# Hybrid mixer tail: first attention group's logits beside the last value panel, products reordered, norm statistics per token tile

## The reference

```python
q, k = rope(cq @ w_q_up), rope(k_att)                 # 8 attention heads of 64
mask = top-64 keys of the index scores, causal        # from idx_score
p   = softmax(where(mask, q k^T / 8, -inf))           # per query and head
att = rms_norm(p @ v, attn_out_norm)                  # norm over each head's 64
W   = exp(decay matrix - row maximum)                 # 4 mLSTM heads of 128
S   = (q_m k_m^T) * 128^-0.5 * W
hm  = (S @ v_m) / max(|sum S|, exp(-M))
hm  = sigmoid(o_m) * rms_norm(hm, mlstm_out_norm)     # norm over each head's 128
y   = concat([att, hm]) @ w_out
```

## Time and profile before

| | us |
|---|---|
| median of 3 runs | 2291.05 (2290.8 to 2296.16) |
| profiled execution, its own time | 2288.99 |
| span of its trace | 2287.2 |
| TensorE busy | 2053.7 (90%) |
| VectorE busy | 1509.9 (66%) |
| ScalarE busy | 899.6 (39%) |

### The profile page before, as it was taken

How to read it: one execution, slowest core, us unless ns; L and a number is a source line. 1 busy time by engine, 2 the same in 40 slices (tenths; PEclk the granted TensorE clock), 3 DMA queues, 4 the chain that set the end, 5 groups by cost and what they waited for, 6 DMA issues and landing times. The chain is left out here.

```text
span 2287.2 us, 40136 instructions
## 1 busy us (share of the span) xinstructions
PE 2053.7 (90%) x16866; PEld 1839.9 (80%) x16866; DVE 1509.9 (66%) x2313; ACT 899.6 (39%) x1331; POOL 140.4 (6%) x231
## 2 busy tenths in 40 slices
PE   5998987999999788799987999797799989878997
PEld 5786865888887676689876999797689979877997
DVE  6866476997775666656635777777576656946444
ACT  3436443322222422322234444555344455544443
POOL 0100000010100011200210000000000000000000
PEclk7999998999999789899997999899799989979999
DMA  8531033555541554000003777332357734313552
GB/s 331 201 124 56 1 111 110 174 198 180 202 170 69 205 177 175 20 3 3 3 20 111 259 277 270 110 135 93 111 194 278 276 114 150 129 56 111 184 183 92
DMA packets 59133, 323.94 MB, mean 142 GB/s; under 512 B 6384, under 2 KB 7536, under 8 KB 32624
## 3 DMA queue, kind: packets, MB, share of 16 engines
q1 hardware_dynamic: 33360, 228.97, 28.1%
q0 software_dynamic: 25344, 92.29, 11.3%
q10 hardware_dynamic: 288, 0.66, 0.1%
HBM read 320.84 MB, written 1.05 MB: 141 GB/s over the span
## 5 line engine op out<-in xcount | busy, mean ns | idle before, releaser
L370 DVE TENSOR_TENSOR w_low<-raw,w_high 128x1024 fp32r<-128x1024 f32 (+1 forms) x408 | 473.1, 1202 | 239.3 <-ACT w_high L362 239.0
L362 ACT ACTIVATE w_high<-raw 128x1024 fp32r<-128x1024 f32 (+1 forms) x408 | 402.1, 1034 | 382.8 <-PE banks L400 374.4
L541 DVE SCALAR_TENSOR_TENSOR mod_rows<-mod_rows,silu_condition 128x1024 f32<-128x1024 f32 x176 | 212.5, 1221 | 50.7 <-DMA mod_rows<-rows_dram 48.0
L398 PE MATMUL banks<-ffn_a_l,w_high 128*128 128x256 f32 x704 | 199.9, 284 | 1.9 <-DVE ffn_hidden L996 1.9
L399 PE MATMUL banks<-ffn_a_h,w_high 128*128 128x256 f32 x704 | 199.2, 283 | 0.0
L400 PE MATMUL banks<-ffn_a_h,w_low 128*128 128x256 f32 x704 | 199.1, 283 | 0.0
L398 PE MATMUL banks<-mlp_a_l,w_high 128*128 128x512 f32 (+1 forms) x512 | 176.8, 345 | 11.7 <-DVE mlp_a_l L683 7.7
L527 POOL DMA_DIRECT2D mod_rows<-rows_dram x176 | 93.2, 530 | 1412.5 <-DVE mod_rows L541 1194.9
L399 PE MATMUL banks<-mlp_a_h,w_high 128*128 128x512 f32 (+1 forms) x512 | 175.6, 343 | 0.0
L400 PE MATMUL banks<-mlp_a_h,w_low 128*128 128x512 f32 (+1 forms) x512 | 175.4, 343 | 0.0
L398 PE MATMUL banks<-mlp_hidden_l,w_high 128*128 128x512 f32 (+1 forms) x512 | 173.4, 339 | 1.3 <-DVE mlp_hidden_l L1004 1.3
(11 more groups left out here) (595 smaller groups left out, 4891.4 us busy)
## 6 DMA issues: line engine op xcount, KB each, us to landing
raw<-panels_dram SPq DMA_DIRECT2D x204, 1024.0 KB, 4.8
mod_rows<-rows_dram POOLq DMA_DIRECT2D x176, 512.0 KB, 5.1
mod_0a_rows<-rows_dram SPq DMA_DIRECT2D x8, 1024.0 KB, 20.0
x_features<-x_features_dram SPq DMA_DIRECT2D x1, 2048.0 KB, 11.2
constants<-small_dram SPq DMA_DIRECT2D x1, 1672.5 KB, 6.8
silu_condition<-conditions_dram SPq DMA_DIRECT2D x2, 512.0 KB, 12.4
out_dram<-x_features SPq DMA_DIRECT2D x4, 256.0 KB, 2.1
constants<-small_dram SPq DMA_DIRECT2D x1, 736.5 KB, 5.1
```

The costliest lines, as they stand in the source:

```text
L362: self.nc.scalar.activation(self.wh[:, m % 2, cols], self.raw[:, slot, cols], ACT.Copy).then_inc(self.w_high, 1)
L370: self.nc.vector.tensor_tensor(self.wl[:, m % 2, cols], self.raw[:, slot, cols], self.wh[:, m % 2, cols].bitcast(F32), ALU.subtract).then_ ...
L398: self.nc.tensor.matmul(out, sh(k), ml(k), start=(opens and k == 0), stop=False)
L541: nc.vector.scalar_tensor_tensor(row if v == nv - 1 else self.scratch[:], row, 1.0, self.cond[v][:], ALU.mult, ALU.mult, accum_out=mod[:, ...
```

## The change

Group 0 of the attention (scores, logits, exponentials) moves from the tail to the second panel of `mix_vm_in`. That stage now uses two PSUM banks instead of four, and its last panel no longer carries the split of the next panel: ScalarE makes that `w_high` explicitly beside it, VectorE makes that `w_low` later, in the tail. In the tail TensorE makes both remaining score groups first, and the value products of the attention's tile 1 before the turning of the mLSTM output. The mLSTM value products are cut by tile. The attention's norm statistics are made for each tile on its own, tile 0 before the mLSTM's. Per layer, that adds six VectorE instructions (five of 8 columns, one sum of 512; the existing ones of 16 columns and 1024 shrink to half) and one ScalarE root of 8 columns; the rest only moves.

```diff
@@ beside the last value panel (beside_last, lines 2787 to 2808 before) @@
+        if which == "pe" and p == 1:
+            for q in (7, 10):
+                eng.wait_ge(*b_info["taken"][q])
+            scores(eng, 0)
         if which == "dve" and p == 1:
             ml_scores(eng)
+            eng.wait_ge(mask_ready, 2)
+            logits(eng, 0)
+        if which == "act" and p == 1:
+            pr.split_upto("act", eng, pr.m)
+            probs(eng, 0)
 
     pr.linear("mix_vm_in", 2, 2, 4, pr.tokens(high, low, 2, PC, KD), vals(vm), [], engines=("act",),
-              prior=b_info, info=vm_info, beside=beside_last)
+              banks=(0, 1), prior=b_info, info=vm_info, beside=beside_last, carry=False)
...
-    bank_s = (0, 2, 0)
-    bank_t = (2, 0, 2)
+    bank_s = (2, 6, 2)
+    bank_t = (6, 2, 6)
+    bank_turn = (4, 5, 0)
+    bank_m = (1, 4)
+    bank_o = (5, 2)
...
@@ TensorE, after the panel @@
+        pe.wait_ge(ml_scored, 8)
+        scores(pe, 1)
+        pe.wait_ge(logits_out, 1)
+        scores(pe, 2)
         for q in range(4):
             pe.wait_ge(*vm_info["taken"][q])
-        pe.wait_ge(mask_ready, 2)
-        scores(0)
-        scores(1)
-        for g, (b, i, j) in enumerate(((4, 0, 0), (5, 1, 0), (6, 1, 1))):
-            pe.wait_ge(ml_scored, 8)
+        for b, i, j in ((bank_turn[0], 0, 0), (bank_turn[1], 1, 0), (bank_turn[2], 1, 1)):
...
-        pe.wait_ge(logits_out, 1)
-        scores(2)
-        pe.wait_ge(m_t_out, 3)
-        for i, bank in enumerate((7, 4)):
...
         pe.wait_ge(logits_out, 2)
         turn_probs(0)
-        values(0, 5)
+        ml_values(0)
+        pe.wait_ge(m_t_out, 2)
+        values(0, bank_o[0])
         pe.wait_ge(logits_out, 3)
         turn_probs(1)
         turn_probs(2)
+        ml_values(1)
+        values(1, bank_o[1])
+        values(2, bank_o[1])
         for i in range(2):
             pe.wait_ge(m_scaled, i + 1)
...
-        values(1, 0)
-        values(2, 0)
         for i in range(2):
             pe.wait_ge(o_scaled, i + 1)
-        for b in range(4):
-            for i in range(2):
+            for b in range(4):
...
@@ ScalarE @@
-        probs(0)
-        for g, b in enumerate((4, 5, 6)):
+        for g, b in enumerate(bank_turn):
             act.wait_ge(m_t_done, g + 1)
             nc.scalar.activation(St[g], ps[:, b, :], ACT.Copy).then_inc(m_t_out, 1)
-        probs(1)
         probs_out(0)
-        squares(m_squared, (m_done, 1), hm_sq[:, 0, :], 7)
-        squares(m_squared, (m_done, 2), hm_sq[:, 1, :], 4)
-        probs(2)
-        pr.split_upto("act", act, pr.m + 1)
+        probs(act, 1)
+        probs(act, 2)
+        squares(m_squared, (m_done, 1), hm_sq[:, 0, :], bank_m[0])
+        squares(o_squared, (o_done, 1), att_sq[:, 0, :], bank_o[0])
         probs_out(1)
         probs_out(2)
+        act.wait_ge(o_summed, 1)
+        nc.scalar.activation(root_a[:, 0], t2[:, 0], ACT.Sqrt, bias=c("eps")).then_inc(o_rooted, 1)
+        squares(m_squared, (m_done, 2), hm_sq[:, 1, :], bank_m[1])
+        pr.split_upto("act", act, pr.m + 1)
         act.wait_ge(m_summed, 1)
         nc.scalar.activation(ml_root, ml_t, ACT.Sqrt, bias=c("eps")).then_inc(m_rooted, 1)
-        squares(o_squared, (o_done, 1), att_sq[:, 0, :], 5)
-        squares(o_squared, (o_done, 2), att_sq[:, 1, :], 0)
+        squares(o_squared, (o_done, 2), att_sq[:, 1, :], bank_o[1])
+        act.wait_ge(o_summed, 2)
+        nc.scalar.activation(root_a[:, 1], t2[:, 1], ACT.Sqrt, bias=c("eps")).then_inc(o_rooted, 1)
...
@@ VectorE @@
+        def att_sums(i):
+            dve.wait_ge(p_ready, 8 * i + 8)
+            ch.then(dve, nc.vector.reciprocal(inv_a[:, i], total[:, i]))
+            dve.wait_ge(o_squared, i + 1)
+            ch.then(dve, nc.vector.tensor_reduce(ss[:, i], att_sq[:, i].rearrange("p (h n) -> p h n", n=64), AX.X,
+                                                 ALU.add))
+            scale(ss[:, i], inv_a[:, i], t2[:, i], ATT_D, o_summed)
...
-        logits(0)
-        logits(1)
-        logits(2)
-        dve.wait_ge(ml_scored, 8)
+        logits(dve, 1)
+        logits(dve, 2)
...
         pr.split_upto("dve", dve, pr.m)
+        att_sums(0)
+        att_scaled(0)
         dve.wait_ge(m_squared, 2)
...
-        dve.wait_ge(p_ready, 16)
-        ch.then(dve, nc.vector.reciprocal(inv_a, total))
         pr.split_upto("dve", dve, pr.m + 1)
         dve.wait_ge(om_sigmoid, 1)
+        att_sums(1)
+        gate_ml((0, 1))
+        att_scaled(1)
+        gate_ml((2, 3))
         for b in range(4):
             dve.wait_ge(y_high, b + 1)
...
```

More of the change, by code:

```diff
@@ L2837, in _ @@
+    pr.linear("mix_vm_in", 2, 2, 4, pr.tokens(high, low, 2, PC, KD), vals(vm), [], engines=("act",),
+              banks=(0, 1), prior=b_info, info=vm_info, beside=beside_last, carry=False)
     @pr.block.tensor
     def _(pe):
-        def scores(g):
-            i, lo, hi = parts[g]
-            w = (i + 1) * P
-            for h in range(lo, hi):
-                at = (h - lo) // 2 * w
-                last = nc.tensor.matmul(ps[:, bank_s[g] + h % 2, at:at + w], qr[half(h), h // 2, i * P:(i + 1) * P],
-                                        pj[half(h), KA + h // 2, 0:w], start=True, stop=True)
-            last.then_inc(s_done, 1)
```

151 lines of the change are left out of this document (80 added, 71 removed).

## The result

| | before | after |
|---|---|---|
| median, us | 2290.93 (2289.3 to 2296.16) | 2263.49 (2261.61 to 2264.57) |
| profiled execution, us | 2288.99 | 2263.13 |
| span of its trace, us | 2287.2 | 2261.3 |
| mean granted TensorE clock | 0.936 | 0.937 |

A forecast was written before the change was run, and what follows sets the result against it. The prediction took a chain of handovers between TensorE, VectorE and ScalarE, with no engine full, as the bound. Two layers at 15.6 us save 31.2: 2288.99 to 2257.8 profiled, plus 2.06 for the median, 2260; range 2254 to 2269.

The forecast's parts named there:

- mLSTM output scaled: VectorE in the tail: the mLSTM scaling ends at 1598.6 instead of 1604.9, 6.3 us sooner.
- attention tile 1 scaled: End of VectorE's deciding chain: tile 1's scaling reaches 1604.05 instead of 1619.77, 15.7 us earlier.
- `mix_out` starts: TensorE begins `mix_out` at 1605.4 instead of 1621.51, paced by the low parts.
- last low part ends, before less after: End of the tail on VectorE: the last low part comes 15.6 us earlier per layer.
- The chain: Handovers between three queues from the value panel to `mix_out`; VectorE's part decides, tile 1's scaling 15.7 us earlier.
- two main terms: Tail: mLSTM root no longer behind copies and exponentials (scaled 6.3 us sooner); tile 1's products no longer behind the turning.
- The values ran at the high clock: TensorE's tile 1 value products taken at 2.4 GHz, 4.0 us not 6.9; low clock would cost about 0.4 us.
- The later load: The moved split starts a later panel's load at 1588.5 instead of 1574; costed at nothing, needed only by `mix_out`'s third.
- rival 2: Value panel: group 0 isn't hidden, everything 2.1 + 1.0 us later, 12.5 us saved per layer, 2266; chance 0.08.
- time saved there is saved in the program: Stretch from value panel's end to `mix_out`: everything behind needs its result, so its 15.6 us per layer count fully.
- rival 3: Low clock lasts through `mix_out`: 180 more slow matmuls cost 16.9 us, 4.4 lost per layer, 2300; chance 0.03.
- 1 (clock falls early in the tail): TensorE at 1.2 GHz from 1585 on slows turnings and values: 12.5 us saved per layer, 2266; chance 0.12.

The follow-up runs named there:

- 2: Changed kernel with attention tile 1's value products back behind the turnings of the mLSTM output: 2275.7 us.
- 5: Kernel before, with only tile 1's value products moved ahead of the turnings of the mLSTM output: 2283.98 us.
- 6: Kernel before, with only the mLSTM root moved on ScalarE, ahead of the split and the two copies: 2283.56 us.
- 1: Changed kernel with group 0's scores, logits and exponentials back at the head of the tail, after the panel: 2264.45 us.
- Experiment 7: Kernel of experiment 4 plus unused products in TensorE's gaps, 6 behind tile 1's values and 2 before the last turnings: 2253.18 us.
- 8: Kernel of experiment 4 with mLSTM sums and root ahead of tile 0's root and scaling, ScalarE's second-panel split behind tile 1's squares: 2249.54 us.
- 3: Changed kernel with the attention's sums, root and scaling made for both tiles together, at tile 1's place: 2262.14 us.
- experiment 4: Changed kernel with VectorE's half of the split of `mix_out`'s second panel behind all low parts: 2257.62 us.
- 9: Changed kernel with 14 unused products in the idle stretch ahead of the sums of the norm before each feed-forward: 2262.73 us.
- 11: Changed kernel with 9 unused products before the feed-forward norm's sums and one before the three products opening the feed-forward's sums: 2263.73 us.
- 10: Kernel of 8 plus unused products: 4 and 2 in the mixer's gaps, 14 ahead of each feed-forward norm's sums: 2253.88 us.
- 12: Kernel of 8 plus the 9 and 1 unused products in the feed-forward stage, none in the mixer: 2256.17 us.

## Why the prediction was right, and where it was off

It named 2260.0 with 2254 to 2269; the median is 2263.49. The window from the panel's end to `mix_out`, forecast at 26 to 27 us, is 25.6. The steps in the order of the prediction, with the changed kernel's times less 1.69 us to put them on the clock of before:

| step | forecast | measured |
|---|---|---|
| group 0's exponentials start | 1576.6 | 1576.51 |
| last value panel ends | 1579.0 | 1579.25 |
| mLSTM output scaled | 1598.6 | 1598.22 |
| attention tile 1 scaled | 1604.05 | 1603.54 |
| `mix_out` starts | 1605.4 | 1604.80 |
| last low part ends, before less after | 15.6 | 16.4 |

**The chain** held to 0.6 us at every step up to `mix_out`'s start and to 0.8 at its end, and its two main terms hold by experiment: the order of the values is worth 7.0 us in the changed kernel (2) and 4.7 alone (5), the root's place 4.4 alone (6). The root's place was not taken back in the changed kernel, so what it is worth there is not shown. The values ran at the high clock, as taken. The later load, costed at nothing, cost nothing: TensorE has no gap in the changed kernel's `mix_out`. Group 0's move was worth 2.4 us to the chain and 1.3 to 1.5 to the segment (1); rival 2 had priced it at 3.1.

**The step that failed** is "time saved there is saved in the program". The last low part came 16.4 us earlier, but the segment shrank by 15.4. After the last low part (ends 1623.64 before and 1608.92 after), VectorE's first copy starts 1.97 us later before and 3.02 later after, and the windows view of the changed kernel shows why:

```profile
1606.50:1611.50 5.00, 5.00 (x23) 5.00 (x24) 3.56 (x9) 1.42 (x4) 0.53 (x1) 0.50 0.02 3
...
1611.70:1623.20 11.50, 11.50 (x99) 11.50 (x98) 5.64 (x8) 4.56 (x6) 0.53 (x1) 1.00 0.38 139
```

The clock was 0.50 until 5.2 us after `mix_out`'s start, in place of 2.1. That is a small form of rival 3, in the matmuls it named; 24 slow matmuls, far below the 134 at which it would have decided. Experiment 7 shows what is to be had there: 1.7 to 1.9 us. Then each feed-forward stage lost 1.5 us. Over two layers that is 2.1 + 3.0 us lost against 1.6 more from the chain than forecast, so 3.5 us; with the 1.7 us by which the first segment began later, the profiled execution should lie 5.2 above its forecast of 2257.8, and it lies 5.3 above (2263.13). That the median misses by only 3.5 is luck: the forecast added 2.06 us from profiled execution to median, and after the change that distance is 0.36. Reading the granted clock behind the mixer too would have shown the place of the 1.5 us and not their size: no row of before says how long a low stretch lasts when the same code is reached at another moment.

**That the 1.5 us are the clock's** is borne out by all 28 feed-forward stages of the 14 kernels in this study, sorted by the low clock of the second stretch, around the opening of the products:

| low clock of the second stretch, us | stages | duration of the stage, us |
|---|---|---|
| 3.4 | 5 (before twice; 1, layer 0; 8 twice) | 202.92 to 202.96 |
| 6.8 | 20 (the changed kernel twice; 2 to 7, 9 and 11; 10 and 12, layer 1) | 203.63 to 204.49 |
| 10.2 | 3 (1, layer 1; 10 and 12, layer 0) | 205.02 to 205.30 |

Within the middle row the stages differ by 0.9 us, and the low stretch ahead, over the norm's sums, doesn't sort them alone. What the low clock costs can be added up, though. In every one of the 28 stages the duration is 194.7 us, plus the time from its start to the first product of the first panel, plus 0.45 for each us of low clock behind that product's start, to within 0.05 us. (The 0.45 is an estimate from starts of matmuls: 0.118 us apart at 1.00 in place of 0.214 at 0.50.) In layer 0 of the changed kernel the three terms of the loss are:

- the norm's sums end later, so that the fourth opening product starts 6.13 us into the stage in place of 5.62: 0.5 us;
- this product takes 2.07 us in place of 1.22: 0.85 us;
- the matmuls behind it held 3.5 us of low clock in place of 3.2: 0.14 us.

Together that is the 1.5 us, a third of it from the first low stretch and the rest from the second. Layer 1 shows the same sum. In 9 the first term is gone and the last is larger (4.0 us of low clock), which makes the 0.3 us gained there. I tried to remove the loss (9 to 12) and didn't succeed, so this part is an account of 28 stages and not an edit with its effect. Why the same code, reached at another moment, is met by 3.4, 6.8 or 10.2 us of low clock is open. The gap ahead of the fourth opening product can't be the cause in general: in 18 of the 28 stages the clock fell before that gap began, and in one (12, layer 0) there is no gap. All 28 falls came 1.9 to 5.5 us after the first of the one-row products had begun.

**Rivals.** 1 (clock falls early in the tail) didn't come: the values took 3.68 us; the clock fell at 1598.07 instead, in the gap before the turnings. On the rule that recent activity releases the clock (the Trainium skill, "TensorE: Matmul & The Clock Gate", "What's actually happening"), the changed kernel's windows above decide as those of before did, only less sharply: TensorE was busy for all of the 5.00 us from 1606.50, at 0.50. Rival 2 priced its case too high (3.1 us, where 1 shows 1.3 to 1.5 in the segment) and did not come: VectorE went to group 0's logits at 1575.49 without idling for the mask, so group 0 was hidden.

## What to carry to other kernels

When several queues wait for each other in turn, list for each wait the work that the waiting queue has behind it and doesn't need the awaited value; here putting the value products ahead of the turnings gave 4.7 us per layer and a root ahead of copies 4.4, each alone in the kernel before, without any work left out. Then look again at the engine that has become gapless (here VectorE) for work nobody waits for: a split of 2.35 us, moved behind the low parts, was worth 2.7 us per layer (experiment 4), and taking the statistic first whose consumer is first 2.7 more (experiment 8), of which 1.0 is the earlier start of `mix_out` and 1.7 the clock that was back by then. A tenth of the gain went back to the clock in an untouched stage (3.0 of 30.8 us), so compare such stages in the two traces before explaining the total by the edit.

## What the runs showed of the hardware

- What low clock costs depends on what it lies over. Over the norm's sums, whose end ScalarE's squares set at the high clock, they took 5.53 us with none (11), 5.53 to 5.97 in a stage with a stretch of 3.4 us, and 6.12 to 6.46 with one of 6.8. The fourth opening product took 1.12 us at 1.00 (8) and 2.07 at 0.50. Over matmuls that follow each other, each us of low clock cost 0.45 us.
- The clock also fell while TensorE was busy: in 12 it went to 0.50 at 1641.71, 15 us after the last idle time over 0.3 us, during products of one row.
- Filling a gap with unused products doesn't reliably keep the clock: it did in the mixer (7: 1.7 to 1.9 us per layer), gave nothing in the mixer of 8 (10), and in the feed-forward it took the first low stretch away and left the second of 6.8 us (9, 11) or left one of 10.2 us in layer 0 (10, 12).
- The same code differs by up to 2.4 us per mixer by the clock alone: `mix_out` starts 39.34 and 39.46 us into layer 1's segment in 8 and 12, yet the segments are 60.34 and 62.74 us. That is as large as several of the edits, so the start of `mix_out` is the better measure of an edit ahead of it. Behind that start the first held no low clock and the second 5.2 us.
- An unused product of 256 plain fp32 columns is two records of 0.22 us at the high clock (18 records in 4.05 us), so 14 of them took 6.2 us (9), 2 us more than the idle stretch that they were to fill.
